# Two activation buffers placed 64 bytes off the 128-byte grid of the weight buffers, in a two-layer hybrid block on one core

## What is computed

```
h    = rms_norm(x, norm1_w);  proj = h @ w_in          # 2048 x 5648
x    = x + concat([attn, ssm]) @ w_out                 # 2048 x 2048
h    = rms_norm(x, norm2_w)
u    = causal_dwconv(h @ w_up)                         # 2048 x 11264
x    = x + (silu(u_gate) * u_val) @ w_down             # 5632 x 2048
h    = rms_norm_2(x, g) * (1 + scale) + shift          # scale, shift, gate from silu(c) @ w_ada
proj = h @ w_in_2                                      # 2048 x 7168
x    = x + gate * (concat([y_a * silu(z_a), y_r * silu(z_r)]) @ w_out_2)
out  = rms_norm_2(x, final_gain)
```

## Time and profile before

| | |
|---|---|
| median of 3 runs | 1691.69 us |
| the profiled execution | 1692.72 us |
| its span, first to last instruction | 1691.1 us |
| mean granted TensorE clock | 0.992 |
| TensorE busy (matmul / weight load) | 97% / 95% |
| VectorE, ScalarE busy | 69%, 48% |
| DMA, mean | 199 GB/s |

### The profile page before, as it was taken

One profiled execution on the slowest core, in us unless ns is written; L12 is line 12 of the kernel. 1 busy time (PEld: TensorE's weight loads), 2 busy tenths in 40 slices (PEclk: granted clock), 3 DMA queues, 4 the chain that ended last, 5 costly groups with the idle time before them and its releaser, 6 DMA issues.

```text
span 1691.1 us, 33703 instructions
## 1 busy us (share of the span) xinstructions
PE 1642.5 (97%) x13254; PEld 1612.7 (95%) x13254; DVE 1161.5 (69%) x1357; ACT 807.0 (48%) x972; POOL 26.2 (2%) x53
## 2 busy tenths in 40 slices
PE   6999999999999999999999999999799999999997
PEld 6998899989999999999999999999799999999997
DVE  5776677675678888888888887667654544664754
ACT  5444345544554544545445454444454643454542
POOL 0000000000000000000000000000000000000000
PEclk9999999999999999999999999999999999999999
DMA  8454344455548777787777775555455555445451
GB/s 320 138 166 137 123 150 138 150 187 176 185 156 331 257 265 285 250 298 262 257 284 260 291 271 197 181 184 182 137 190 184 183 182 166 134 158 167 152 168 50
DMA packets 85043, 336.17 MB, mean 199 GB/s; under 512 B 9440, under 2 KB 9696, under 8 KB 78560
## 3 DMA queue, kind: packets, MB, share of 16 engines
q1 hardware_dynamic: 77328, 281.34, 48.8%
q0 software_dynamic: 7056, 51.38, 8.4%
q10 hardware_dynamic: 576, 2.24, 0.4%
HBM read 332.82 MB, written 2.10 MB: 198 GB/s over the span
## 4 chain that ended last, share of the span: by engine, by line
PE 72%; DVE 5%; issue 1%; ACT 1%; DVEq 0%; ACTq 0%
PE PS L1084 23%; PE PS L1086 23%; PE PS L1088 23%; DVE ada_w L919 1%; DVE wlo L575 1%; ACT whi L251 1%; PE PS L1186 1%; DVE UV L877 1%; PE PS L1153 1%; PE PS L1330 0%; DVE X L1071 0%; PE PS L1172 0%; DVE rb L609 0%; DVE X L591 0%; PE PS L1131 0%
## 5 line engine op out<-in xcount | busy, mean ns | idle before, releaser
L1084 PE MATMUL PS<-gh,whi 128*128 128x256 f32 x3520 | 1012.9, 288 | 19.6 <-DVE wlo L575 14.5
L1088 PE MATMUL PS<-gh,wlo 128*128 128x256 f32 x3520 | 998.6, 284 | 0.0
L1086 PE MATMUL PS<-gl,whi 128*128 128x256 f32 x3520 | 998.4, 284 | 0.0
L575 DVE TENSOR_TENSOR wlo<-raw,whi 128x1024 fp32r<-128x1024 f32 x528 | 645.0, 1224 | 460.3 <-ACT whi L251 458.0
L251 ACT ACTIVATE whi<-raw 128x1024 fp32r<-128x1024 f32 x528 | 557.2, 1058 | 763.6 <-PE PS L1088 762.1
L1084 PEld LDWEIGHTS PS<-gh,whi 128*128 128x128 f32 x3520 | 678.1, 193 | 27.3 <-issue 24.8
L1086 PEld LDWEIGHTS PS<-gl,whi 128*128 128x128 f32 x3520 | 678.1, 193 | 2.8 <-issue 1.9
L1088 PEld LDWEIGHTS PS<-gh,wlo 128*128 128x128 f32 x3520 | 677.7, 193 | 0.0
L1084 PE MATMUL PS<-ah,whi 128*128 128x256 f32 x704 | 198.9, 283 | 8.8 <-DVE UV L877 5.2
L1086 PE MATMUL PS<-al,whi 128*128 128x256 f32 x704 | 197.6, 281 | 0.0
L1088 PE MATMUL PS<-ah,wlo 128*128 128x256 f32 x704 | 197.3, 280 | 0.0
(11 more groups left out here) (186 smaller groups left out, 803.9 us busy)
## 6 DMA issues: line engine op xcount, KB each, us to landing
raw<-weights SPq DMA_DIRECT2D x528, 512.0 KB, 3.4
ada_w<-w_ada POOLq DMA_DIRECT2D x48, 1024.0 KB, 5.1
X<-xT SPq DMA_DIRECT2D x4, 512.0 KB, 11.9
outT<-X SPq DMA_DIRECT2D x4, 512.0 KB, 2.6
c<-const ACTq DMA_DIRECT2D x1, 1536.0 KB, 6.3
c_act<-c_rows POOLq DMA_DIRECT2D x1, 1024.0 KB, 9.4
prm<-params SPq DMA_DIRECT2D x1, 276.5 KB, 3.7
mask<-const ACTq DMA_DIRECT2D x1, 256.0 KB, 9.4
```

What stands on the lines that cost most here:

```text
L575: dve.tensor_tensor(wlo[:, j % SPLIT, :], raw[:, j, :], whi[:, j % SPLIT, :].bitcast(F32), ALU.subtract).then_inc(s_lo, 1)
L1084: pe.matmul(out[:, t, :], whi[:, b, w], hi[:, kt, :], start=first and half == 0 and t % 2 == 0, stop=False, skip_group_check=True)
L1086: pe.matmul(out[:, t, :], whi[:, b, w], lo[:, kt, :], start=False, stop=False, skip_group_check=True)
L1088: mm = pe.matmul(out[:, t, :], wlo[:, b, w], hi[:, kt, :], start=False, stop=last and half == 1, skip_group_check=True)
```

## The change

The running offset is moved on by 64 bytes ahead of `gh` and by another 64 behind `gl`:

```
         raw, _ = place("raw", [P, RAW, 1024])
         whi, _ = place("whi", [P, SPLIT, 1024], F32R)
         wlo, _ = place("wlo", [P, SPLIT, 1024], F32R)
+        at[0] += 64
         gh, _ = place("gh", [P, DT, S], F32R)
         gl, _ = place("gl", [P, DT, S], F32R)
+        at[0] += 64
         prm, _ = place("prm", [P, N_PARAMS])
```

## The result

The change made the kernel 1.8% faster: 1661.95 us median of 4 runs (1661.47 to 1663.56) against 1692.88 us for the kernel before on the same chip, a ratio of 0.9816 with a 95% interval of 0.9803 to 0.9828. The forecast was 1663 us. The span fell from 1691.1 to 1659.8 us.

A forecast was written before the change was run, and what follows sets the result against it. TensorE was taken as the bound, its time being the number of matmuls times their start distance. Gains of 22.9 + 6.7 less 0.4 us make 29 us, from 1692.7 us profiled or 1.0 lower by median to 1663 us; range 1612 to 1675.

The forecast's parts named there:

- What bounds the kernel: Whole kernel: TensorE is busy 97% of the span; shortening the matmuls' start distance shortens the time almost one for one.
- That the start offset relative to the weights sets the distance: Matmuls on gh and gl: sharing the weights' offset modulo 128 gives 120 ns, an offset of 64 gives 117.8 or 113.3.
- The rival of no change: Matmuls on gh and gl: the distance has another reason and stays 120.0 ns, 1692 us; chance 0.11.
- the reading by region: Within no change: gh's place 80 KB higher in the partition, not its offset, sets the distance; no chance of its own.
- The main term: 10,400 matmuls on gh and gl go from 120.0 to 117.8 ns, 2.2 ns each: 22.9 us gained.
- The second term: Second input projection, beginning at 1.2 GHz: 1500 matmuls at 113.3 ns give another 4.5 ns each, 6.7 us.
- With the same place on the grid: cost nothing: Everything behind gl moves 128 bytes up, which was taken to cost nothing.
- The sign named for this: FFN rounds: the down product's matmuls stay at 117.8 ns.
- The wait ahead of the second down group: Eight FFN rounds: 0.05 us a round turns into TensorE waiting, 0.4 us given back.
- The better lock everywhere: Rival: matmuls on gh, gl and also ah hold 113.3 ns, 75 us gained, 1616 us; chance 0.16.
- the slower rival: Matmuls on gh and gl lock at up to 123 ns, 31 us lost, 1723 us; chance 0.05.

The follow-up runs named there:

- run with 256: Against the kernel before, gh, gl and all buffers behind them moved 256 bytes up: 1693.88 us, ratio 1.0002.
- run with 128: Against the kernel before, gh and gl moved 128 bytes up, everything behind them where the change has it: 1678.11 us, ratio 0.9912.
- place 96: Against the kernel before, gh and gl moved to 96 relative to the weights, ah and al at 192: 1688.64 us, ratio 0.9971.
- the best layout tried: Against the kernel before, gh, gl and the FFN buffers ah, al, ah2, al2 all at 192 to the weights: 1649.39 us, ratio 0.9738.

## Why the prediction was right, and where not

**What bounds the kernel** was right, and it is the step that carried the forecast: nearly all of what the matmuls' distance changed went into the time. The run with 256 has the old distances and the old time; the run with 128 would save 10,400 x 1.3 + 2100 x 2.4 ns = 18.6 us by its distances and saved 15.2.

**That the start offset relative to the weights sets the distance** was right. The rival of no change fell with the change itself, and the reading by region with two runs: 256 bytes further up in memory give 120.0 again, and moved weights give the 117.8 of moved activations. The sentence of the Trainium skill that was weighed in the prediction ("TensorE: Matmul & The Clock Gate", on what each phase is for) was taken in the prediction to mean that the start offset can't matter. The offset does matter: the places of the two operands relative to each other move the distance between 113.3 and 120.0 ns. Whether the sentence itself fails here is open: that it is the weight load which the stream meets was argued, and is still only argued; no run isolates the load.

**The main term**, 10,400 x 2.2 ns, was right for most of the kernel: 117.8 in the first output projection, in the FFN and in the long stretch of the second input projection. Ahead of the first down product stand 3648 matmuls on `gh` and `gl`, 3648 x 2.2 = 8.0 us, measured 7.8.

**The second term was wrong in its place; two thirds of its size came back elsewhere, by luck.** The second input projection began at the low clock and was expected at 113.3; it is at 117.8 (1276 records in 150 us), so the 6.7 us are not there. (The clock was up from 1228.7 us there, not from 1237, so the term as meant was 0.3 us larger.) That the rise of the clock sets the good state came from a single stretch. It doesn't: in the last run (all moving buffers at 192) the matmuls ahead of that wait, on `ah`, were at 113.3 ns and those on `ah2` behind the low clock at 117.8, the reverse of before:

```profile
L1090 PE MATMUL PS<-ah,wlo x32: 276/276/276, 1145.8 to 1156.4; 128*128 128x256 f32 x32
L1090 PE MATMUL PS<-ah,wlo x28: 280/281/281, 1174.9 to 1184.5; 128*128 128x256 f32 x28
```

What came instead in the kernel after lies at full clock behind small matmuls: the last 1100 matmuls on `gh` and `gl`, from 1510 us on, which are the end of the second input projection and the second output projection, are at 113.8 on the mean. At 4 ns below the forecast that is 4.4 us.

**The buffers behind `gl` were not free.** "With the same place on the grid: cost nothing" rested on a grid of 128 bytes. It is 256, so the 128 bytes moved `ah` from 64 to 192, and its mean went from 117.4 to 114.5 ns: 2100 x 2.9 = 6 us gained that stood nowhere in the sum. They keep their offset modulo 128, as is said of the change, but not modulo 256. The sign named for this, a down product still at 117.8 in the rounds, did not come.

**The wait ahead of the second down group** was right in kind and too small, for the same reason. The row of waits was 5.2 us in 8 before; after the change it is

```profile
PE PS L1086 <- DVE UV L879: 7.3, 8, 0.9
```

2.1 us more instead of 0.4. The chain through ScalarE and VectorE took 543.88 - 534.74 = 9.14 us and takes 536.22 - 527.08 = 9.14 us now, while 48 matmuls on `ah` within it became up to 4.5 ns shorter each, 0.22 us a round:

```profile
527.08 1.07 ACT whi L253
534.96 1.15 DVE UV L879
536.22 0.38 PE PS L1086
```

Together: 7.8 + 12.1 + 11.4 = 31.3 us, against a forecast of 8 ahead of the first down product, 7 from there to the end of the last one and 14 behind. The total is good to some 2 us because the errors had opposite signs: 6.7 us that did not come and 1.7 more of waiting, against 6 on `ah` and 4.4 from 1510 us on.

**The better lock everywhere** didn't come with this change, though it exists in parts of it. The slower rival did not happen with the change, and a state worse than 120 on the mean was in none of the runs; 125 ns occurs as one of a cycle whose mean is 120.0 (place 96).

## What to carry to other kernels

Where TensorE is the bound and the profile shows a matmul distance above its columns over the clock, compare the distance between stretches that read different buffers: a difference between them is a clue to placement, and a few bytes of padding test it. Compute the places modulo more than the suspected grid before calling a shift neutral; here 128 bytes ahead of `ah` were worth 6 us. Do the scan instead of one step, and judge a layout by several executions, because one place can have two steady states.

## What I had not expected of the hardware

- The distance depends on the relative start of moving and stationary operand modulo 256 bytes: 120.0 at 0 and 256, mostly 116.7 at 32, 118.7 at 128, down to 113.3 at 64 and 192, for 256 columns in float32r at a granted clock of 1.00.
- It is not a fixed cost but a cycle: at 0 every distance is 120; at 64 distances of 117 to 119 with a mean of 117.8; at 96 six distances from 116 to 125 with a mean of 120.0; at 128 a cycle of five with 118.7.
- At 64 and 192 two states live side by side, 117.8 and 113.3, and other places have two as well (117.3 and 118.7 at 160). The stream keeps its state over 1500 matmuls and more, and from one buffer to another at the same place, and can change it where TensorE stops or one start is late by 25 ns. What picks the state there stays open, and with it how to hold 113.3 throughout, which by my estimate of 10,400 x 6.7 + 2100 x 4.1 ns would be about 78 us less than before; the best layout tried has 44.
- With `gh` at 192 and `gl` at 64 neither was ever at 113.3 in the one trace taken, although each place has that state alone.
